# Eight recurrent heads: projections in three passes on split weights, and the level queries multiplied on GpSimd

## The reference

```python
def gla_chunked(q, k, v, logf, s0):
    ...
        b = jnp.cumsum(fc, axis=2)
        o_inter = jnp.einsum('bhtd,bhde->bhte', qc * jnp.exp(b), state)
        rel = b[:, :, :, None, :] - b[:, :, None, :, :]
        decay = jnp.where(tril, jnp.exp(jnp.minimum(rel, 0.0)), 0.0)
        scores = jnp.einsum('bhtd,bhsd,bhtsd->bhts', qc, kc, decay)
        o = o_inter + jnp.einsum('bhts,bhse->bhte', scores, vc)
...
        pq, pff, pfb, pi, pg, pa, pb, pgh, pgc = split_proj(h @ w_in[l])
```

## Time and profile before

| | us |
|---|---|
| median of 3 runs | 3535.61 (3535.46 to 3536.98) |
| the profiled execution: its time, its span | 3541.43, 3539.7 |
| TensorE busy over the span | 3341.1 (94%) |
| VectorE, ScalarE, GpSimd busy | 1617.0 (46%), 1049.0 (30%), 1531.3 (43%) |
| mean granted TensorE clock | 0.967 of 2.4 GHz |
| head projections and heads 0 to 7 | from 2408.0 to 2787.0 in the span |

### The profile page before, as it was taken

How to read it: one execution, slowest core, us unless ns; L and a number is a source line. 1 busy time by engine, 2 the same in 40 slices (tenths; PEclk the granted TensorE clock), 3 DMA queues, 4 the chain that set the end, 5 groups by cost and what they waited for, 6 DMA issues and landing times. The chain is left out here.

```text
span 3539.7 us, 40630 instructions
## 1 busy us (share of the span) xinstructions
PE 3341.1 (94%) x14988; PEld 2526.2 (71%) x14988; DVE 1617.0 (46%) x2751; ACT 1049.0 (30%) x1996; POOL 1531.3 (43%) x873
## 2 busy tenths in 40 slices
PE   8999999999879989999999999988999899889998
PEld 7886987777653867766368878775555687668886
DVE  4751003443422055554321163433888699737741
ACT  2112113333314134444320011554666400321111
POOL 6764663434312334431056656650001265446664
PEclk9999999999979889999999999999999899999999
DMA  4233221111115212113533223221111122122321
GB/s 156 97 102 110 92 93 56 64 60 62 52 36 161 66 60 68 67 57 101 180 124 113 96 78 110 94 87 54 48 48 48 48 95 90 66 72 96 101 95 55
DMA packets 84487, 297.19 MB, mean 84 GB/s; under 512 B 9441, under 2 KB 10977, under 8 KB 84162
## 3 DMA queue, kind: packets, MB, share of 16 engines
q1 hardware_dynamic: 80352, 286.34, 24.5%
q10 hardware_dynamic: 3250, 5.77, 0.5%
q0 software_dynamic: 688, 2.49, 0.2%
HBM read 289.32 MB, written 2.10 MB: 82 GB/s over the span
## 5 line engine op out<-in xcount | busy, mean ns | idle before, releaser
L596 POOL TENSOR_SCALAR arena_r<-ring 128x1024 fp32r<-128x1024 f32 x430 | 463.2, 1077 | 1871.0 <-PE psum L608 1249.5
L606 PE MATMUL psum<-arena_r,arena_r 128*128 128x512 f32 (+2 forms) x3120 | 1239.3, 397 | 34.5 <-DVEq L2982 13.4
L607 PE MATMUL psum<-arena_r,arena_r 128*128 128x512 f32 (+2 forms) x3120 | 1207.2, 387 | 0.0
L608 PE MATMUL psum<-arena_r,ring_r 128*128 128x512 f32 (+1 forms) x3088 | 1196.6, 388 | 0.0
L598 POOL TENSOR_TENSOR ring_r<-ring,arena_r 128x1024 fp32r<-128x1024 f32 x430 | 1058.0, 2460 | 64.7 <-issue 10.0
L606 PEld LDWEIGHTS psum<-arena_r,arena_r 128*128 128x128 f32 x3120 | 594.9, 191 | 176.7 <-issue 41.6
L607 PEld LDWEIGHTS psum<-arena_r,arena_r 128*128 128x128 f32 x3120 | 595.1, 191 | 122.6 <-issue 9.7
L608 PEld LDWEIGHTS psum<-arena_r,ring_r 128*128 128x128 f32 x3088 | 584.6, 189 | 119.5
L2358 PE MATMUL psum<-arena,ring 128*128 128x512 f32 x512 | 234.6, 602 | 14.4 <-ACT arena L2433 14.4
L1155 DVE SCALAR_TENSOR_TENSOR arena<-arena,con,psum 128x512 f32<-128x512 f32 x64 | 47.8, 747 | 422.9 <-PE psum L1097 422.9
L2358 PEld LDWEIGHTS psum<-arena,ring 128*128 128x128 f32 x512 | 94.6, 194 | 114.3 <-issue 114.3
(11 more groups left out here) (389 smaller groups left out, 4245.1 us busy)
## 6 DMA issues: line engine op xcount, KB each, us to landing
ring<-in_weights SPq DMA_DIRECT2D x534, 512.0 KB, 3.3
arena<-arena ACTq DMA_DIRECT2D x20, 128.0 KB, 3.4
arena<-in_x_t SPq DMA_DIRECT2D x8, 256.0 KB, 6.3
out_t<-arena SPq DMA_DIRECT2D x8, 256.0 KB, 2.2
arena<-in_w_ck POOLq DMA_DIRECT2D x1, 1024.0 KB, 7.9
arena<-in_w_cv POOLq DMA_DIRECT2D x1, 1024.0 KB, 10.1
arena<-in_ln_bc ACTq DMA_DIRECT2D x1, 1024.0 KB
arena<-in_ctx_t ACTq DMA_DIRECT2D x1, 1024.0 KB, 7.3
```

Of the source, the lines that this page charges most:

```text
L596: nc.gpsimd.tensor_scalar(hi_part(t), src, 1.0, 1.0, ALU.mult, ALU.mult)
L606: nc.tensor.matmul(out, w_hi, a_hi, start=start, stop=False)
L607: nc.tensor.matmul(out, w_hi, a_lo, start=False, stop=False)
L608: return nc.tensor.matmul(out, w_lo, a_hi, start=False, stop=stop)
```

## The change

The head tiles are now split as well. `to_split` covers all 40 tiles of the stage. ScalarE makes the high halves (`high(j)`, an `ACT.Copy` of 128 by 1024), three before the first gates, three more while head 0 is prepared, and then one in each of steps 0, 2, 4 and 6 of a head, tile 4*hd+6+i/2 in step i, 26 in all. GpSimd makes the low half of the same tile in the same step. `project_half` waits for the split and issues `three` for each slice. In `fill` the query multiplication is gone from VectorE; GpSimd does it for each level, waiting for that level's exponential, and `scores` waits for it (`lev_q_done`).

```diff
--- before.py
+++ after.py
@@ -580,9 +580,8 @@
         def lo_part(t):
             return ring_r[t % RING][:, 0:1024]
 
-        def halve_tiles(pool, t0, n, by_act=()):
-
-            highs = 0
+        def halve_tiles(pool, t0, n, by_act=(), highs=0):
+
             for t in range(t0, t0 + n):
                 i = split_no[t]
                 src = ring[:, t % RING * 1024:(t % RING + 1) * 1024]
@@ -2120,7 +2119,7 @@
             T0 = w_at[0]
             H0 = T0 + 8
             END = H0 + 32
-            to_split(T0, H0 - T0)
+            to_split(T0, END - T0)
             n_hi, n_lo = singles(16, KT), singles(24, KT)
             ctx_hi, ctx_lo, gates_c = context_tiles()
             vx = tiles(32, KT)
@@ -2139,6 +2138,7 @@
             @block.gpsimd
             def _(pool):
                 halve_tiles(pool, T0, H0 - T0)
+                halve_tiles(pool, H0, 6, range(H0, END))
 
             @block.vector
             def _(dve):
@@ -2293,7 +2293,7 @@
                                                       sem("gla_sc_done"))
             picked, copied = sem("gla_picked"), sem("gla_copied")
             out_done, sq_done, var_done, rt_done = sem("gla_out_done"), sem("gla_sq_done"), sem("gla_var_done"), sem("gla_rt_done")
-            head_done = sem("gla_head_done")
+            head_done, lev_q_done = sem("gla_head_done"), sem("gla_lev_q_done")
             PART = {"f": 0, "b": 1, "q": 2, "g": 3}
 
             def halves(ap, level):
@@ -2352,19 +2352,20 @@
                     t = H0 + 4 * hd + PART[part]
                     b = PART[part] % 2
                     if half == 0:
-                        pe.wait_ge(w_in[t % RING], 16 * (t // RING + 1))
+                        pe.wait_ge(w_split, split_no[t] + 1)
                         bank_take(pe, b)
+                    w_hi, w_lo = parts_of(t)
                     for k in range(4 * half, 4 * half + 4):
-                        last = nc.tensor.matmul(psum[:, b], slot(t % RING)[:, k], hn[:, k], start=(k == 0),
-                                                stop=(k == KT - 1))
+                        last = three(psum[:, b], w_hi[:, k], w_lo[:, k], n_hi[k], n_lo[k], k == 0, k == KT - 1)
                     if half:
                         last.then_inc(w_used, 1)
 
                 def scores(s):
                     b = 2 + s % 2
+                    hd, i = divmod(s, NS)
                     pe.wait_ge(lev_done, s + 1)
+                    pe.wait_ge(lev_q_done, s - s // NS + (i < NS - 1))
                     bank_take(pe, b)
-                    hd, i = divmod(s, NS)
                     for c in range(4):
                         rhs = q_s[:, hd % 2, chunk(c)] if i == NS - 1 else lev[s % 3][:, 1, chunk(c)]
                         last = nc.tensor.matmul(psum[:, b, chunk(c)], lev[s % 3][:, 0, chunk(c)], rhs, start=True,
@@ -2421,6 +2422,20 @@
                         if hd + 1 < KT:
                             project_half(hd + 1, "fbqg"[i // 2], i % 2)
 
+            @block.gpsimd
+            def _(pool):
+                for hd in range(KT):
+                    for i in range(NS - 1):
+                        n = NS * hd + i
+                        if i == 0:
+                            pool.wait_ge(q_in, hd + 1)
+                        pool.wait_ge(exp_done, n - n // NS + 1)
+                        nc.gpsimd.tensor_tensor(lev[n % 3][:, 1], lev[n % 3][:, 1], q_s[:, hd % 2], ALU.mult)
+                        pool.drain().then_inc(lev_q_done, 1)
+                        j = 4 * hd + 6 + i // 2
+                        if i % 2 == 0 and j < 32:
+                            halve_tiles(pool, H0 + j, 1, (H0 + j,), j)
+
             @block.scalar
             def _(act):
                 def gates(hd, part):
@@ -2448,6 +2463,13 @@
                     act.wait_ge(w_used, H0 + 4 * hd + 4)
                     nc.scalar.activation(g_s[:, hd % 2], psum[:, 1], ACT.Silu).then_inc(bk_free[1], 1)
                     act.drain().then_inc(gate_in, 1)
+
+                def high(j):
+                    t = H0 + j
+                    act.wait_ge(w_in[t % RING], 16 * (t // RING + 1))
+                    act.wait_ge(w_used, split_tiles[split_no[t] - NHI] + 1)
+                    nc.scalar.activation(hi_part(t), ring[:, t % RING * 1024:(t % RING + 1) * 1024], ACT.Copy)
+                    act.drain().then_inc(w_hi_in, 1)
 
                 def level_exp(s):
                     act.wait_ge(diff_done, s - s // NS + 1)
@@ -2500,10 +2522,15 @@
                     last.then_inc(bk_free[b], 1)
                     act.drain().then_inc(copied, 1)
 
+                for j in range(3):
+                    high(j)
                 gates(0, "f")
+                high(3)
                 gates(0, "b")
+                high(4)
                 logs(0)
                 query(0)
+                high(5)
                 gate_silu(0)
                 level_exp(0)
                 level_exp(1)
@@ -2527,6 +2554,8 @@
                             keys(hd, i - 5)
                         if i in (6, 7):
                             copy_far(s - 1)
+                        if i % 2 == 0 and 4 * hd + 6 + i // 2 < 32:
+                            high(4 * hd + 6 + i // 2)
                         if hd + 1 < KT:
                             if i == 4:
                                 gates(hd + 1, "f")
@@ -2570,6 +2599,7 @@
                     dve.drain().then_inc(kd_done, 1)
 
                 def decayed_queries(hd):
+                    dve.wait_ge(q_in, hd + 1)
                     dve.wait_ge(q_exp, hd + 1)
                     for t in range(2):
                         nc.vector.tensor_tensor(qd[:, t], qd[:, t], q_s[:, hd % 2], ALU.mult)
@@ -2597,15 +2627,12 @@
                 def fill(s):
 
                     hd, level = divmod(s, NS)
-                    if level == 0:
-                        dve.wait_ge(q_in, hd + 1)
                     dve.wait_ge(exp_done, s - s // NS + 1)
                     lo, hi = halves(lev[s % 3][:, 0], level)
                     f_lo = halves(k_s[0][:, hd % 2], level)[0]
                     b_hi = halves(k_s[1][:, hd % 2], level)[1]
                     nc.vector.tensor_tensor(lo, lo, f_lo, ALU.mult)
                     nc.vector.tensor_tensor(hi, hi, b_hi, ALU.mult)
-                    nc.vector.tensor_tensor(lev[s % 3][:, 1], lev[s % 3][:, 1], q_s[:, hd % 2], ALU.mult)
                     dve.drain().then_inc(lev_done, 1)
 
                 def diagonal(s):
```

## The result

The changed kernel took 3599.51 us (3598.11 to 3601.56, 4 runs), the kernel before 3536.21 (3535.46 to 3536.98, 4 runs) beside it: ratio 1.0179 [1.0167, 1.0192], slower by 63.3 us. The forecast was 3590.6. The profiled execution took 3598.19, its span 3596.5, its mean granted clock is 0.958.

What follows compares the result with a forecast made beforehand. TensorE paced the heads; afterwards a chain of waits would. Terms 3.5 + 6.1 + 40.3 + 5.1 = 55.0 us on the profiled 3541.4 gave 3596.4, so 3590.6 on the median; 8 in 10 for 3550 to 3628.

Steps and rivals of the forecast that it cites:

- two surcharges: On top of each head's 47.8 us chain: 2.4 us for GpSimd and VectorE blocking each other, 1.3 for TensorE's slower clock.
- start of the stage: Before head 0: f starts 6.8 us late, four tiles give back 5.2, the lower clock costs 1.9; together +3.5 us.
- head 6: Head with two tiles only: less for the third high, behind T6 and in surcharges; 47.6 us against 42.5, +5.1.
- head 7: Head without projections, at VectorE's pace: 0.7 less a level against a GpSimd multiplication of 1.24; 0, between -4 and +3.
- T0→T1: Scores of step 0 to scores 1: squares, high, low and GpSimd multiplication in a chain, 10.4 us instead of 7.0.
- T6→T0': Scores 6 to the next head's scores 0: fourth high behind `copy_far`, then low and multiplication, 9.5 us instead of 10.1.
- T1→T3: Scores 1 to scores 3: high, low and multiplication follow level 4's exponential and `query_decays`, 11.5 us instead of 9.5.
- T3→T6: Scores 3 to scores 6: third high ahead of the gates delays q by 1.2 us; 16.4 us instead of 15.9.
- Sharing: In the heads GpSimd and VectorE hold each other up; 2.4 us a head taken, from bounds of 0 and 20.
- Faster: Rival: highs and lows run a step ahead, no score waits; heads of 39.6 us, about 3514 us, chance 0.09.
- Milder: Rival: no surcharge, GpSimd's work falls into gaps and the clock stays up; heads of 47.8 us, 3561 us, chance 0.23.
- no change: Rival: within 0.2% of before (7 us), needing heads of 43.5 us, without `squares` and `query_decays` in the chain; chance 0.03.

Runs made afterwards that it cites:

- e3: Changed kernel with each low half one or two multiplications later in GpSimd's queue: 3577.53 us, ratio 1.0118 to the kernel before.
- e1: Changed kernel with the query multiplication back on VectorE, three-pass projections, highs and lows kept: 3566.64 us, ratio 1.0084 to the kernel before.
- e7: e1 without the low halves of 26 tiles (third product uses the high half twice), GpSimd idle in the heads: 3549.75 us, ratio 1.0038 to the kernel before.
- e4: Changed kernel without the low halves of the 26 tiles split inside the heads (third product uses the high half twice): 3553.59 us, ratio 1.0052 to the kernel before.
- e8: Changed kernel with three filler matmuls on TensorE before the waits of steps 1, 3 and 4: 3586.85 us, ratio 1.0144 to the kernel before.
- e10: Kernel before the change with plain head projections on 416 of 512 columns, no splitting in their place: 3522.57 us, ratio 0.9965 to the kernel before.
- e9: Changed kernel with plain head projections, query multiplications on GpSimd except in head 7, there on VectorE: 3535.09 us, ratio 1.0001 to the kernel before.
- e12: e9 with the tail's first three tiles split one at a time in heads 5 and 6: 3539.28 us, ratio 1.0012 to the kernel before.

## Why the prediction was right, and where its sizes were off

Slower, by the named mechanism, and inside the range: the measured head of 51.2 us is the predicted 51.5, and its chain is the predicted one. That the two surcharges came so near is in part luck: 2.4 was a choice between 0 and 20, and the 1.3 for the clock was too small. By its terms, from the two profiled executions:

| term | predicted | measured |
|---|---|---|
| start of the stage | +3.5 | +6.3 |
| head 0 | +6.1 | +7.2 |
| heads 1 to 5 | +40.3 | +38.9 |
| head 6 | +5.1 | +7.8 |
| head 7 | 0 | +4.2 |
| tail | 0 | -1.8 |
| sum | 55.0 | 62.6 |

(From T0 of head 1 on, 256.15 against 217.24 us in heads 1 to 5, 50.34 against 42.51 in head 6; the stage began 5.8 us earlier in the changed kernel's trace, the last `key_turn` at 2401.9 against 2407.7, and the profiled executions differ by 56.8. So the profiled execution of the kernel before had lost these 5.8 ahead of the stage, and to take them off the forecast for the median was right; the medians differ by 63.3.)

- *The chain of a head.* T0→T1 10.2 for 10.4, T6→T0' 9.7 for 9.5: right to 0.2. T1→T3 took 12.7 for 11.5 and T3→T6 18.7 for 16.4; these hold 3.4 of the 3.7 us that "two things on top" put beside the chain. 51.2 for 51.5. In T3→T6 the term too small is the way to the gates: q started at T3 + 9.3 for 8.4.
- *The queue order.* Held: moving the lows two multiplications back was worth 2.9 us a head (e3).
- *Sharing.* The 2.4 stood for lows and multiplications together, and no run measures that by itself. With the multiplications on VectorE, the lows cost 2.8 us a head (e1 less e7). The one-sided costs do not make the whole: lows alone +2.8, multiplications alone +1.1 (e4 less e7), both +8.1 (51.23 less 43.15). Of the 4.1 beyond the sum, e3 recovers 2.9 by the order alone. The rest was not separated, and the clock moves with every version (mean of heads 1 to 5: 0.91 changed, 0.90 e1, 0.95 e4, 0.94 e7).
- *The clock.* 1.9 us a head (e8), for 1.3.
- *Start: mis-sized, 2.8 us.* f started 6.9 us late, for 6.8. Four tiles that "give back 5.2" less 1.9 for the clock are 3.3; from f's first matmul to the last short matmuls ahead of head 0 (L2396, now L2397, 2440.03 and 2438.21) it took 29.2 us after and 32.0 before, 2.8 less. The step that failed stands behind them: "The level 0 multiplication on GpSimd takes the place of VectorE's at about the same time", with no term for the sixth low half. From those short matmuls to T0 it took 15.6 us for 13.3, because the low half held a scan of VectorE (2.50 us for 0.40) and the multiplication held L2634 (1.29 for 0.43).

```profile
2406.59 2.35 POOL L597 TENSOR_TENSOR ring_r<-ring,arena_r 128x1024 fp32r<-128x1024 f32 x1 [28.07 <-ACTq L2472]
...
2409.04 0.79 PE L605 MATMUL psum<-arena_r,arena_r 128*128 128x512 f32 x1 [6.88 <-POOLq L598]
...
2445.63 2.35 POOL L597 TENSOR_TENSOR ring_r<-ring,arena_r 128x1024 fp32r<-128x1024 f32 x1 [16.94 <-ACTq L2472]
...
2445.77 2.50 DVE L2587 TENSOR_TENSOR_SCAN arena<-arena 128x128 f32<-128x128 f32 x1
...
2453.80 2.05 PE L2371 MATMUL psum<-arena 128*128 128x128 f32 x8 [12.74 <-DVEq L2636]
```

The idle time ahead of T0 (10.44 us in the earlier trace rows) does not stop shorter tiles from paying. In e10, with no split tile, f started at 2403.19 and T0 came 40.2 us later, for 45.3 before, behind the same idle time:

```profile
2443.37 2.05 PE L2370 MATMUL psum<-arena 128*128 128x128 f32 x8 [10.44 <-issue]
```

- *Head 7: mis-sized, 4.2 us.* The 4.9 us "between T6 of head 7 (2782.07) and the tail (2786.96)", for "one split takes some 3.8", put the splits behind T6. GpSimd is done with level 6 already in step 4, since exponentials run two steps ahead, and the time is lost beside these splits, in T3→T6 (19.4 us for 15.4), while T0→T3 is no longer than before. In e9, with the splits in head 6 and the multiplications back on VectorE, T3→T6 of head 7 takes 15.1 and the head 30.9.
- *Head 6: mis-sized, 2.7 us.* "1.8 less of the two surcharges" did not come; T0→T1 and T1→T3 of that head, with two highs and lows still in them, took 11.2 and 12.7, for 10.2 and 12.7 in the mean of heads 1 to 5.

The Trainium skill ("SBUF — State Buffer", section "Who interferes with whom") says that a VectorE instruction in a two-port mode excludes GpSimd, that one with two inputs in SBUF excludes a GpSimd instruction that reads SBUF, and that the later one fully blocks. The trace agrees: the held instructions end 0.3 to 0.6 us after the subtraction beside them, whether they have 256 columns (2.58 for 0.42) or 1024 in a `tensor_scalar` (2.60 for 0.69). So the price of such a hold goes by GpSimd's instruction, not by VectorE's.

*The rivals.* "Faster" was wrong in more than its order of queues. It let T3→T6 stay at 16.4 while the steps ahead of it shrink; e10 and e7 show that the part grows as TensorE comes to T3 earlier, to 17.3 and 19.5. From the version with free splitting to the change, a head goes 41.1, 43.2 (e7, with ScalarE's copies), 46.0 (low halves, e1), 51.2 (multiplications on GpSimd). That the 2.1 between the first two is the copies' place in ScalarE's queue is argued from e7's trace and was not separated from the three-pass form of the matmuls. "Milder" (heads of 47.8) is about what e3 reached by the order of GpSimd's queue, and "no change" (43.5) what e7 reached without the lows.

## What to carry to other kernels

Before shortening the engine that paces a loop, ask how long the chain behind it is. Here TensorE had 5.1 us a head less to do even with splitting for nothing (e10), and a head gained only 1.4, since the chain of VectorE and ScalarE then set T3→T6.

Price a helper's instruction twice: by what stands behind it in its own queue, and by the one instruction of the other engine that it holds up. Each price counts only if what is held is on the chain. The same split cost 0.4 us in one step and 4 to 5 us in another.

Idle time ahead of an instruction does not tell whether shorter work before it pays. If the wait starts when that work ends, as ahead of T0 in e10, the whole of the gain arrives.

## What the runs showed that was not expected

- A GpSimd subtraction of 2.34 us beside one VectorE instruction of 0.42 made head 5 of e12 3.9 us longer up to T6: 2.2 of blocking, and 1.8 because TensorE, idle for 4.01 us instead of some 1.8, then ran a half projection in 5.37 us for 3.60, with a granted clock of 0.72 over 2686 to 2692 us, so at the 1.2 GHz level for part of it.
- The costs of two kinds of helper work on one in-order engine did not add: 2.8 us a head for the low halves alone, 1.1 for the multiplications alone, 8.1 together.
